# A decoder trunk on one core: the feed-forward activation turned by VectorE blocks and regrouping transfers in place of TensorE

## The reference

```python
h = rms_norm(x, ffn_pre_gain[l])
gt, up = jnp.split(h @ w_ffn_in[l], 2, axis=-1)
x = x + rms_norm((jax.nn.silu(gt) * up) @ w_ffn_out[l], ffn_post_gain[l])
```

## Time and profile before

| what | value |
|---|---|
| median of three runs | 1546.94 us (1545.62 to 1546.96) |
| profiled execution | 1543.52 us |
| its span, first to last instruction | 1541.9 us |
| granted TensorE clock, mean | 0.995 |
| busy: PE, DVE, ACT, POOL | 99%, 59%, 50%, 2% |
| weight units through the ring | 531 whole, one in halves |
| read from HBM | 294.19 MB, 192 GB/s over the span |

### The profile page before, as it was taken

The page is one execution under the profiler, slowest core; times in us unless marked ns, Lnnn a source line. Parts: engine busy times, 40 slices in busy tenths (PEclk is TensorE's granted clock), DMA queues, the critical chain, the costliest instruction groups (busy, mean ns, idle before and its releaser), DMA issues.

```text
span 1541.9 us, 20320 instructions
## 1 busy us (share of the span) xinstructions
PE 1520.7 (99%) x6934; PEld 1254.4 (81%) x6934; DVE 911.8 (59%) x1094; ACT 771.0 (50%) x945; POOL 29.2 (2%) x49
## 2 busy tenths in 40 slices
PE   9999999999999999999989999999999999999996
PEld 6887887888888888888878888888888888888885
DVE  7878998654445677567565454455444544444444
ACT  7645545665566444566556444444444444344342
POOL 0000000000000000000000000000000000000001
PEclk9999999999999999999999999999999999999998
DMA  9655555655555657765436555555555556565563
GB/s 337 230 184 182 178 178 177 198 180 169 180 176 169 233 184 257 262 198 191 145 123 203 193 187 187 186 189 192 189 190 190 189 181 218 195 195 194 191 192 108
DMA packets 82106, 296.89 MB, mean 193 GB/s; under 512 B 9168, under 2 KB 9424, under 8 KB 81040
## 3 DMA queue, kind: packets, MB, share of 16 engines
q1 hardware_dynamic: 80096, 285.12, 56.6%
q0 software_dynamic: 1536, 10.75, 1.9%
q10 hardware_dynamic: 432, 0.45, 0.1%
HBM read 294.19 MB, written 2.10 MB: 192 GB/s over the span
## 4 chain that ended last, share of the span: by engine, by line
PE 98%; DVE 1%; DMA 0%; ACT 0%; SPq 0%; issue 0%; DVEq 0%; ACTq 0%
PE acc L1282 18%; PE acc L1284 18%; PE acc L1283 17%; PE side L1282 11%; PE side L1284 11%; PE side L1283 11%; PE tr L1284 3%; PE tr L1283 3%; PE tr L1282 3%; PE tr L1299 1%; DMA raw<-in_units 0%; DVE xres L1263 0%; PE side L1338 0%; PE tr L1345 0%; PE side L1363 0%; PE side L1394 0%
## 5 line engine op out<-in xcount | busy, mean ns | idle before, releaser
L763 DVE TENSOR_TENSOR w_lo<-raw,w_hi 128x1024 fp32r<-128x1024 f32 x531 | 649.7, 1225 | 575.6 <-ACT w_hi L417 570.6
L417 ACT ACTIVATE w_hi<-raw 128x1024 fp32r<-128x1024 f32 x531 | 562.1, 1060 | 675.9 <-PE acc L1284 356.7
L1282 PE MATMUL acc<-w_hi,xT_hi 128*128 128x512 f32 x860 | 338.9, 394 | 1.4 <-DVE w_lo L763 1.4
L1284 PE MATMUL acc<-w_hi,xT_lo 128*128 128x512 f32 x860 | 335.4, 390 | 0.0
L1283 PE MATMUL acc<-w_lo,xT_hi 128*128 128x512 f32 x860 | 335.1, 390 | 0.0
L1282 PEld LDWEIGHTS acc<-w_hi,xT_hi 128*128 128x128 f32 x860 | 161.8, 188 | 36.6 <-issue 3.3
L1284 PEld LDWEIGHTS acc<-w_hi,xT_lo 128*128 128x128 f32 x860 | 161.6, 188 | 34.1
L1283 PEld LDWEIGHTS acc<-w_lo,xT_hi 128*128 128x128 f32 x860 | 161.8, 188 | 32.5
L1282 PE MATMUL side<-w_hi,xT_hi 128*128 128x512 f32 x480 | 187.1, 390 | 0.0
L1283 PE MATMUL side<-w_lo,xT_hi 128*128 128x512 f32 x480 | 186.8, 389 | 0.0
L1284 PE MATMUL side<-w_hi,xT_lo 128*128 128x512 f32 x480 | 186.8, 389 | 0.0
(11 more groups left out here) (325 smaller groups left out, 1495.7 us busy)
## 6 DMA issues: line engine op xcount, KB each, us to landing
raw<-in_units SPq DMA_DIRECT2D x531, 512.0 KB, 3.4
x_tok<-in_x SPq DMA_DIRECT2D x4, 512.0 KB, 5.9
xres<-in_x POOLq DMA_DIRECT2D x1, 2048.0 KB, 10.1
m_raw<-in_mem_t POOLq DMA_DIRECT2D x1, 2048.0 KB, 8.4
mq<-in_mem POOLq DMA_DIRECT2D x1, 2048.0 KB, 15.2
x_raw<-in_x_t SPq DMA_DIRECT2D x7, 256.0 KB, 6.3
out<-xres SPq DMA_DIRECT2D x3, 512.0 KB, 2.9
post_gain<-in_mix_post_gain POOLq DMA_DIRECT2D x1, 1024.0 KB, 18.9
```

The lines of the kernel that those rows point to most:

```text
L417: a_.activation(w_hi[:, j % RING], raw[:, j % RING], ACT.Copy).then_inc(hi_ready, 1)
L763: v_.tensor_tensor(w_lo[:, s], raw[:, s], w_hi[:, s].bitcast(F32), ALU.subtract).then_inc(lo_ready, 1)
L1282: pe.matmul(bank(b, h), hi[:, kt, tok], w_hi[:, s, k], start=begin, stop=False)
L1284: mm = pe.matmul(bank(b, h), lo[:, kt, tok], w_hi[:, s, k], start=False, stop=end)
```

## The change

The transposes on PE and their two copies go. In their place, per chunk:

- DVE, step 1 (`hidden_turn`): two instructions turn `hb` in blocks of 32x32 within each group of 32 partitions, one per half of the tokens, into `h_blk`;
- GpSimd (`spread_blocks`): 16 transfers, one for each pair of source group b and destination group a of 32 partitions, 32 partitions x 2 x 512 B each, from `h_blk` to `hT_st`, where every block stands on its partitions; it first waits for the blocks and for `hT_lo` of the chunk before;
- ACT, step 12 (`hidden_hi`): waits for all 16, then copies `hT_st` to `hT_hi` in one instruction;
- DVE, step 13 (`hidden_lo`): `hT_lo` as the difference, in one instruction.

`hT_st` and `h_blk` take 4 KB per partition each, in space that is free in this part. PE waits for `hT_ready` 10 at the start of the output phase and for 11 before its unit 20.

```diff
--- before.py
+++ after.py
@@ -59,7 +59,7 @@
 U_XO, U_FI, U_FO, U_END = 260, 268, 444, 532
 G_S5, G_PRE, G_PROJ, G_MID, G_GLU, G_GATE, G_BR, G_OUT, G_MK, G_XQ, G_MV, G_XO, G_FI, G_FO = (
     0, 1, 4, 12, 13, 15, 23, 35, 39, 40, 41, 42, 46, 68)
-T_GLU, T_BR, T_X1, T_X2, T_FFN = 0, 2, 10, 18, 26
+T_GLU, T_BR, T_X1, T_X2 = 0, 2, 10, 18
 
 N_X, N_GM, N_Y1, N_MEM, N_X1, N_Y2, N_X2, N_Y3 = range(8)
 
@@ -199,6 +199,8 @@
         hT_lo = at("hT_lo", 124, [FFN // P, SEQ], F32R)
         silu_g = at("silu_g", 168, [HALVES, NC])
         hb = at("hb", 172, [HALVES, NC])
+        hT_st = at("hT_st", 176, [HALVES, 4, 4, 32])
+        h_blk = at("h_blk", 196, [HALVES, 4, 4, 32])
         yg3 = at("yg3", 48, [HALVES, D])
         post_gain3 = at("post_gain3", 64, [D])
 
@@ -262,6 +264,8 @@
         mg_ready, xres_landed, gain_landed, mq_landed, m_raw_landed, mq_squared = (
             sem("mg_ready"), sem("xres_landed"), sem("gain_landed"), sem("mq_landed"), sem("m_raw_landed"),
             sem("mq_squared"))
+        h_blocked = sem("h_blocked")
+        hT_turned, hT_hi_ready, hT_ready = sem("hT_turned"), sem("hT_hi_ready"), sem("hT_ready")
         squared, x1_ready, x2_ready = sem("squared"), sem("x1_ready"), sem("x2_ready")
         k_turned, kx_ready, q_turned, qx_ready = sem("k_turned"), sem("kx_ready"), sem("q_turned"), sem("qx_ready")
         xz_done, xmax_ready, xexp_done, xp_ready, p_turned, pT_ready, xo_done, xo_hi, xo_lo = (
@@ -389,6 +393,19 @@
             for h in range(HALVES):
                 pool.wait_ge(acc_taken[h], G_OUT + 4)
             g.dma_start(post_gain[:], xattn_post_gain[0:1].to_broadcast([P, D])).then_inc(gain_landed, 16)
+            def spread_blocks(i):
+
+                pool.wait_ge(h_blocked, i)
+                if i > 1:
+                    pool.wait_ge(hT_ready, i - 1)
+                for a in range(4):
+                    for b in range(4):
+                        g.dma_start(hT_st[32 * a:32 * a + 32, :, b].rearrange("p h k c -> p h (k c)"),
+                                    h_blk[32 * b:32 * b + 32, :, a].rearrange("p h k c -> p h (k c)")).then_inc(hT_turned, 16)
+
+            spread_blocks(1)
+            for i in range(2, 12):
+                spread_blocks(i)
             pool.wait_ge(unit_used, U_FO)
             g.dma_start(post_gain3[:], ffn_post_gain[0:1].to_broadcast([P, D])).then_inc(gain_landed, 16)
 
@@ -457,6 +474,13 @@
                                                  tr[:, b, k * SEQ:(k + 1) * SEQ], ACT.Copy,
                                                  scale=cols[:, bass.ds(k0 + (gain + 2 * b + k), 1)])
                     last.then_inc(turn_hi, 1)
+
+            def hidden_hi(i):
+
+                act.wait_ge(hT_turned, i * 256)
+                ks = bass.ds(i * 4 - 4, 4)
+                a_.activation(hT_hi[:, ks].rearrange("p k (g c) -> p k g c", c=32),
+                              hT_st[:].rearrange("p h b k c -> p k (h b) c"), ACT.Copy).then_inc(hT_hi_ready, 1)
 
             def root(n, k):
 
@@ -718,8 +742,8 @@
                         square_quarter(N_X2, j - 1, 24 + 2 * j)
                     if first and j == 6:
                         root(N_X2, 6)
-                    if not first and j == 3:
-                        turn_hi_parts(i * 2 + (T_FFN - 2), hT_hi, i * 4 - 4)
+                    if not first and j == 12:
+                        hidden_hi(i)
                     if j == 7:
                         if first:
                             act.wait_ge(rstd_ready, 7)
@@ -735,8 +759,8 @@
             preload(3, ACT.Sqrt)
             for n in range(4):
                 for j in range(22 * n, 22 * n + 22):
-                    if j == 2:
-                        turn_hi_parts(T_FFN + 20, hT_hi, 40)
+                    if j == 12:
+                        hidden_hi(11)
                     if j == 22 * n + 21:
                         square(G_FO + n, U_FO + j, N_Y3, n, 34 + 2 * n, n % 2)
                     split(U_FO, U_FO // RING, j + RING)
@@ -783,6 +807,24 @@
                                 cols[:, bass.ds(k0 + (gain + 2 * b + k), 1)],
                                 dst_hi[:, ks].rearrange("p k t -> p (k t)").bitcast(F32), ALU.mult, ALU.subtract)
                     last.then_inc(turn_lo, 1)
+
+            def hidden_turn(i):
+
+                for h in range(HALVES):
+                    dve.wait_ge(acc_taken[h], i * 2 + G_FI)
+                for h in range(HALVES):
+                    last = v_.transpose(h_blk[:, h].rearrange("p a k c -> p k a c"),
+                                        hb[:, h].rearrange("p (k a c) -> p k a c", k=4, a=4))
+                last.then_inc(h_blocked, 1)
+
+            def hidden_lo(i):
+
+                dve.wait_ge(hT_hi_ready, i)
+                ks = bass.ds(i * 4 - 4, 4)
+                v_.tensor_tensor(hT_lo[:, ks].rearrange("p k (g c) -> p k g c", c=32),
+                                 hT_st[:].rearrange("p h b k c -> p k (h b) c"),
+                                 hT_hi[:, ks].rearrange("p k (g c) -> p k g c", c=32).bitcast(F32),
+                                 ALU.subtract).then_inc(hT_ready, 1)
 
             def inverse(n, width, squares):
 
@@ -1227,8 +1269,10 @@
                         turn_lo_parts(T_X2 + 4 + j, xT_hi, xT_lo, 8 + 2 * j, C_FFN)
                     if first and j == 5:
                         inverse(N_X2, D, 34)
-                    if not first and j == 3:
-                        turn_lo_parts(i * 2 + (T_FFN - 2), hT_hi, hT_lo, i * 4 - 4)
+                    if not first and j == 1:
+                        hidden_turn(i)
+                    if not first and j == 13:
+                        hidden_lo(i)
                     if j == 15:
                         if first:
                             dve.wait_ge(rstd_ready, 7)
@@ -1247,8 +1291,10 @@
 
             for n in range(4):
                 for j in range(22 * n, 22 * n + 22):
-                    if j == 2:
-                        turn_lo_parts(T_FFN + 20, hT_hi, hT_lo, 40)
+                    if j == 1:
+                        hidden_turn(11)
+                    if j == 13:
+                        hidden_lo(11)
                     if j == 22 * n + 21:
                         if n == 0:
                             dve.wait_ge(gain_landed, 48)
@@ -1516,14 +1562,8 @@
 
 
             def ffn_in(i, first):
-                def step(j):
-                    if j == 2:
-                        for h in range(HALVES):
-                            pe.wait_ge(acc_taken[h], i * 2 + G_FI)
-                        turn(i * 2 + (T_FFN - 2), hb[:])
-
                 if not first:
-                    chunk(i * 16 + U_FI, 0, i * 2 + G_FI, CU, xT_hi, xT_lo, step, lag=2)
+                    chunk(i * 16 + U_FI, 0, i * 2 + G_FI, CU, xT_hi, xT_lo, lag=2)
                 chunk(i * 16 + U_FI, CU, i * 2 + (G_FI + 1), CU, xT_hi, xT_lo, b=1, lag=2)
 
             ffn_in(0, True)
@@ -1531,17 +1571,11 @@
                 ffn_in(i, False)
 
 
-            def last_step(j):
-                if j == 1:
-                    for h in range(HALVES):
-                        pe.wait_ge(acc_taken[h], G_FO)
-                    turn(T_FFN + 20, hb[:])
-
-            pe.wait_ge(turn_lo, T_FFN + 20)
+            pe.wait_ge(hT_ready, 10)
             for n in range(4):
-                chunk(U_FO, 22 * n, G_FO + n, 20, hT_hi, hT_lo, last_step, last=False, b=n % 2, lag=2)
+                chunk(U_FO, 22 * n, G_FO + n, 20, hT_hi, hT_lo, last=False, b=n % 2, lag=2)
                 if n == 0:
-                    pe.wait_ge(turn_lo, T_FFN + 22)
+                    pe.wait_ge(hT_ready, 11)
                 chunk(U_FO, 22 * n + 20, G_FO + n, 2, hT_hi, hT_lo, first=False, k0=20 * UK, b=n % 2)
 
 
```

## The result

| | before | change |
|---|---|---|
| median | 1546.28 us (1544.74 to 1546.96, 4 runs) | 1534.06 us (1533.83 to 1535.46, 4 runs) |
| ratio, 95% interval | | 0.9926 [0.9912, 0.994] |
| profiled execution | 1543.52 us | 1534.13 us |
| its span | 1541.9 us | 1532.5 us |

The change is 12.2 us faster by these medians and 9.4 us by the two profiled executions. The forecast was 9.8 us and 1537.1 us; the time lies inside the range (1534.0 to 1540.5) by 0.06 us only. Which of the two differences is the change's own was the first question for the experiments. One later run of the kernel before took 1920.23 us at a mean granted clock of 0.751 and is left out of the ratios.

What follows compares the result with a forecast made beforehand. The prediction took PE to bound the kernel: eleven turns off PE save 9.8 us, all added work costs 0. From the median 1546.94 us it forecast 1537.1 us, range 1534.0 to 1540.5.

Steps and rivals of the forecast that it cites:

- What bounds the kernel: Whole kernel: PE, busy 1520.7 of 1541.9 us and 98% of the chain; ACT, DVE and loads run ahead.
- The removal: Eleven turns of eight transposes leave PE, 0.89 us each, 9.8 us gained; ends of the term 8.7 and 11.3 us.
- The block transposes: DVE, behind its step 0: two of 128x512 per chunk, 0.7 us each, 1.2 us as upper end, cost 0.
- Transfers: GpSimd, 16 per chunk: issues take 8.6 us, the last landing 2.5 us more, regrouped 11.1 us after the blocks.
- ACT's and DVE's steps: `hT_hi` on ACT at 1.06 us and `hT_lo` on DVE at 1.225 us, both fitting idle time, cost 0.
- The cover: Regrouped data may come up to 33.5 us after the blocks are ready; fails at 1.94 us per transfer.
- DMA traffic: DMA engines: a chunk's regroup is 1024 pieces of 512 B, at a loop share of 0.59; cost 0.
- The slower rival: GpSimd transfers run one after another, ACT stands at step 12: 1608 us, or about 1679; late regroup's chance 0.09.
- its formula: Late-regroup rival's iteration length: 6.6 + 40 + 3.4 = 50.0 us in place of 43.52, 71 us lost over eleven.
- DVE's hold-off: Late regroup by another road: GpSimd issues each wait two DVE splits, about 1724 us in all; chance 0.02.
- the ring: Weight slots before PE: a split ends 5.6 us before PE wants it, which hides lateness of ACT.

Runs made afterwards that it cites:

- the repeated sets: The changed kernel unaltered, measured twice more against the kernel before: 1534.81 us against 1544.11, ratio 0.9944; 1535.34 against 1544.47, ratio 0.9938.
- three regroups: The changed kernel with each chunk's whole regroup made three times, each after the one before had landed: 1587.67 us, ratio 1.0274.
- the two versions: Changed kernel plus three mixer turns off PE: PE waiting for the third chunk at the output projection's start, 1538.13 us; for the second only, 1532.08 us.

## Why the prediction was right, point by point

- **What bounds the kernel:** PE, in both profiles 99% busy and 98% of the chain. Right.
- **The removal, 11 x 0.89 = 9.8 us:** right. From the first matmul of the loop to the end of the span the two profiles take 1541.9 - 844.91 = 696.99 and 1532.5 - 845.55 = 686.95 us, 10.0 apart, 0.91 per turn; the repeated sets gave 9.3 and 9.1, the turns put back 9.8. The starts of the matmuls on both sides of a turn gave the price; the group's record (1.03) would have been 1.5 us too high in the sum.
- **The block transposes, 0.7 us each:** 0.69, the lower end.
- **Transfers, 0.54 us apart and 2.5 to landing:** 0.54 and 2.8. In the two runs with the copy moved earlier, where ACT waits for it, a regroup takes 10.0 to 13.7 us from the blocks to ACT's copy, 11.0 (copy at step 3) and 12.2 (step 4) in the mean, against 11.1.
- **ACT's and DVE's steps at the price of dense ones:** right, so the blocks of 32 cost nothing.
- **The cover, 33.5 us:** right; ACT may stand 6.0 to 6.5 us (6.2 in the sum) before PE feels it. What the sum left out is that far past the edge the loss exceeds the lateness, by the lower clock behind PE's stops: ACT's mean wait of 17.3 us (190.1 / 11) with transfers one by one is 11.1 over the edge and costs 13.9 us an iteration.
- **DMA traffic, 0:** right at once and, in the loop, at twice the amount.
- **The slower rival:** its mechanism held once it was made real, and its formula nearly (57.4 us per iteration with transfers one by one), though it knew nothing of the clock; in the change itself issues do not wait for landings. DVE's hold-off was not there.
- **The predicted time** was 3.0 us too high: 2.4 to 2.8 of them by the median that the forecast started from, 1546.94, where the sets that followed had 1544.1 to 1544.5. Against these it would have read 1534.3 to 1534.7.
- **The range** held by luck. Its own sum ended at 1534.3 us, above the measured 1534.06. It was widened to 1534.0 for stalls, which could only have made the kernel slower and give no reason for a lower bound. The mechanism and the difference of 9.8 us don't hang on this: the repeated sets gave 1534.81 and 1535.34.

## What to carry to other kernels

Where one engine's rows follow one another without a gap, an instruction on it costs the distance that it opens between its neighbours' starts, and a longer detour over idle engines is free as long as the data comes back before the pipeline's slack ends: count that slack from a row (here 27.3 us until the consumer asks, 6 more in the ring). Keep a distance to its edge, since a stopped stage also delays the loads behind it and PE's matmuls can run at the lower clock behind a stop (1.5 us lost behind 4.0 us in the mixer). When a step is moved off the bound engine, look at the first consumer's wait: asking only for the chunk needed first was worth more than the turns themselves in the mixer (6.0 us between the two versions, the clock's part with it, against 2.7 for the turns).

## What the runs showed of the hardware

Without having expected it: DVE's and ACT's reads of 128x1024 in blocks of 32 elements ran as fast as dense ones (1.22 and 1.04 us). Sixteen transfers of 32 KB leave GpSimd 0.54 us apart whatever their landing (1.7 to 3.8 us), and twice the small pieces raised the weights' landing from 3.3 to 4.2 us. After 13.84 us without work PE's matmuls came 0.43 us apart, the lower clock level, until 3.15 us later. The length of the stop alone does not settle it: with three regroups a stop of 2.0 us was followed by such matmuls and one of 2.9 us was not.
